# The masks of a relative bias, made by three engines instead of one, and the order of the work around them

## The reference

```python
c_act = jax.nn.silu(c)
mod = c_act @ ada_w[l] + ada_b[l]                 # 2048 -> 6 * 2048
sh_a, sc_a, g_a, sh_f, sc_f, g_f = jnp.split(mod, N_MOD, axis=-1)
h = modulate(rms_norm(x, attn_pre_norm[l]), sh_a, sc_a)      # h * (1 + sc_a) + sh_a
...
proj = h @ w_in                                    # the first large product
...
rel = positions[:, None, :] - pq[:, :, None]       # key position - query position
bias = jnp.take(bias_tab, t5_bucket(rel), axis=0)  # 32 buckets, 8 heads
s1 = (dq1 @ dk1) * DIFF_SCALE + bias               # and s2 likewise
```

## Time and profile before

| | before |
|---|---|
| median of 3 executions | 1926.73 us |
| lowest, highest | 1925.74, 1927.43 us |
| the profiled execution | 1925.74 us, its span 1924.0 us |
| busy: PE, PEld, DVE, ACT, POOL | 1772.4, 1703.6, 1242.0, 879.2, 215.9 us |
| mean granted clock of TensorE | 0.959 of full speed |
| read from memory | 372.85 MB, 195 GB/s over the span |

### The profile page before, as it was taken

One profiled execution on the slowest core, in us unless ns is written; L12 is line 12 of the kernel. 1 busy time (PEld: TensorE's weight loads), 2 busy tenths in 40 slices (PEclk: granted clock), 3 DMA queues, 4 the chain that ended last, 5 costly groups with the idle time before them and its releaser, 6 DMA issues.

```text
span 1924.0 us, 33456 instructions
## 1 busy us (share of the span) xinstructions
PE 1772.4 (92%) x13960; PEld 1703.6 (89%) x13960; DVE 1242.0 (65%) x1747; ACT 879.2 (46%) x1448; POOL 215.9 (11%) x126
## 2 busy tenths in 40 slices
PE   3799988879979999999999999999699999978997
PEld 3699986869969999999999999999599999856797
DVE  7798889473577757767767656655644446565544
ACT  8444334543445445445445445444444443464432
POOL 0243440003430000000000000000200000161000
PEclk7799999998979999999999999999899999998998
DMA  9797688446936656666656655554155554441151
GB/s 386 262 377 296 243 300 263 134 139 213 341 146 206 226 190 223 222 200 226 220 195 230 217 178 186 186 164 153 49 184 186 183 176 158 142 132 44 39 170 56
DMA packets 102822, 377.13 MB, mean 196 GB/s; under 512 B 11536, under 2 KB 11664, under 8 KB 102544
## 3 DMA queue, kind: packets, MB, share of 16 engines
q1 hardware_dynamic: 102672, 374.99, 57.2%
HBM read 372.85 MB, written 2.10 MB: 195 GB/s over the span
## 4 chain that ended last, share of the span: by engine, by line
issue 46%; PE 37%; DVE 12%; ACT 3%; POOL 1%; DMA 1%; SPq 0%; ACTq 0%; DVEq 0%; POOLq 0%
PE ps L509 10%; PE ps L510 10%; PE ps L511 10%; DVE ada_acc L1190 5%; DVE probs L1301 2%; ACT masks L966 1%; DVE stats L1275 1%; PE ps L591 1%; PE ps L547 1%; PE ps L540 1%; DVE w_lo L1175 1%; POOL probs L1669 1%; PE ps L625 1%; PE ps L610 1%; ACT w_hi L862 1%
## 5 line engine op out<-in xcount | busy, mean ns | idle before, releaser
L509 PE MATMUL ps<-h_hi,w_hi 128*128 128x256 f32 x3264 | 944.7, 289 | 22.4 <-DVE h_lo L1242 10.5
L510 PE MATMUL ps<-h_lo,w_hi 128*128 128x256 f32 x3264 | 930.2, 285 | 0.0
L511 PE MATMUL ps<-h_hi,w_lo 128*128 128x256 f32 x3264 | 929.9, 285 | 0.0
L1175 DVE TENSOR_TENSOR w_lo<-raw,w_hi 128x1024 fp32r<-128x1024 f32 x448 | 553.3, 1236 | 377.3 <-ACT w_hi L862 375.2
L862 ACT ACTIVATE w_hi<-raw 128x1024 fp32r<-128x1024 f32 x512 | 538.7, 1057 | 424.6 <-PE ps L511 404.8
L509 PEld LDWEIGHTS ps<-h_hi,w_hi 128*128 128x128 f32 x3264 | 632.7, 194 | 29.1 <-issue 15.8
L510 PEld LDWEIGHTS ps<-h_lo,w_hi 128*128 128x128 f32 x3264 | 633.8, 194 | 1.1
L511 PEld LDWEIGHTS ps<-h_hi,w_lo 128*128 128x128 f32 x3264 | 633.2, 194 | 0.0
L1190 DVE SCALAR_TENSOR_TENSOR ada_acc<-raw,c_act,ada_acc 128x1024 f32<-128x1024 f32 x180 | 257.9, 1457 | 2.1 <-DMA raw<-in_ada 1.9
L1676 POOL TENSOR_TENSOR w_lo<-raw,w_hi 128x1024 fp32r<-128x1024 f32 x64 | 171.9, 2693 | 471.6 <-ACT w_hi L862 471.6
L509 PE MATMUL ps<-g_hi,w_hi 128*128 128x256 f32 x704 | 201.1, 286 | 3.7 <-DVE g_lo L1513 3.7
(11 more groups left out here) (199 smaller groups left out, 1335.0 us busy)
## 6 DMA issues: line engine op xcount, KB each, us to landing
raw<-in_weights SPq DMA_DIRECT2D x512, 512.0 KB, 3.9
raw<-in_ada SPq DMA_DIRECT2D x192, 512.0 KB, 5.1
x<-in_x SPq DMA_DIRECT2D x1, 2048.0 KB, 17.3
out_y<-x SPq DMA_DIRECT2D x4, 512.0 KB, 2.6
consts<-in_consts SPq DMA_DIRECT2D x1, 863.5 KB, 6.3
params<-in_params SPq DMA_DIRECT2D x1, 593.5 KB, 3.8
probs<-in_pos_q SPq DMA_DIRECT2D x1, 128.0 KB, 2.1
probs<-in_pos_k SPq DMA_DIRECT2D x1, 32.0 KB, 2.4
```

What stands on the lines that cost most here:

```text
L509: nc.tensor.matmul(out, wh, hi[:, k, :], start=start, stop=False)
L510: nc.tensor.matmul(out, wh, lo[:, k, :], start=False, stop=False)
L511: last = nc.tensor.matmul(out, wl, hi[:, k, :], start=False, stop=stop)
L1175: V.tensor_tensor(w_lo[:, h % W_SLOTS, :], raw[:, raw_slot("w", h), :], w_hi[:, h % W_SLOTS, :].bitcast(F32), ALU.subtract).then_inc(lo_dv ...
```

## The change

It makes the same bias in another way. A mask is now 1 where the distance is at or past the start and 0 elsewhere, so the starts are whole numbers, the steps are no longer halved and the added column is gone. The 64 keys are split in eight blocks of eight. For blocks 0 to 4 ScalarE writes the distances in float32 (`distances`, 128x256 each, into the two halves of the later `bias`) and GpSimd compares a block with zero (128x2048). For blocks 5 to 7 VectorE compares `start` with the negated key positions in one instruction of 128x2048 (`last_masks`), set after items 1, 2 and 4 of the modulation. TensorE takes the squares of x first, then waits for the mean of x, for the exponential and for the masks, and makes the bias sums in the order 0, 3, 1, 2. ScalarE's eight `bias_out` all stand behind the root. VectorE's `lo(0)` stands behind the first `modulate`. (`lo(H_IN + 1)`, also taken out, was empty on VectorE: that half is GpSimd's.)

```diff
@@ tensor @@
-            def bias_sums(i):
-                pe.wait_ge(bias_mask, i + 1)
...
+            mean_square("x0", KT)
+            pe.wait_ge(bias_delta, 1)
+            pe.wait_ge(lam_exp, 1)
+            pe.wait_ge(mean_ready, 1)
+            for i in BIAS_GROUPS:
+                if i == 3:
+                    pe.wait_ge(last_mask, 2)
+                elif i == 2:
+                    pe.wait_ge(last_mask, 3)
+                    pe.wait_ge(bias_mask, POOL_MASKS)
+                else:
+                    pe.wait_ge(bias_mask, 2 * i + 2)
+                for qt in range(0, 2):
...
-            for i in range(3):
-                bias_sums(i)
-            pe.wait_ge(lam_exp, 1)
-            bias_sums(3)
-            pe.wait_ge(bias_ready, 6)
-            mean_square("x0", KT)
             pe.wait_ge(bias_ready, 8)
             mod_sum(0)
@@ scalar @@
-            def signs(i):
-                for k in range(16 * i, 16 * i + 16):
-                    last = nc.scalar.activation(masks[:, k, :], start, ACT.Sign, bias=pos_k[:, k:k + 1])
-                last.then_inc(bias_mask, 1)
+            def distances(b):
+                if b >= 2:
+                    act.wait_ge(bias_mask, b - 1)
+                for k in range(8):
+                    last = nc.scalar.activation(distance[b % 2][:, k, :], start, ACT.Identity,
+                                                bias=pos_k[:, 8 * b + k:8 * b + k + 1])
+                last.then_inc(distance_ready, 1)
+            act.wait_ge(start_ready, 1)
+            distances(0)
+            distances(1)
+            act.wait_ge(angle_ready, 1)
+            nc.scalar.activation(cs1[:, :, :], cs1[:, :, :], ACT.Sin).then_inc(cs_ready, 1)
+            distances(2)
+            act.wait_ge(inputs_loaded[4], 16)
+            squares("x0", KT, lambda k: x[:, k, :])
+            distances(3)
+            distances(4)
+            act.wait_ge(lam_sum, 1)
+            nc.scalar.activation(lam[:, 2:4], ps[:, OUT + 1, 0:2], ACT.Exp).then_inc(lam_exp, 1)
+            root("x0")
+            act.wait_ge(bias_mask, POOL_MASKS)
+            for n in range(8):
                 act.wait_ge(bias_summed, n + 1)
...
@@ vector @@
+            chain.link(V.tensor_scalar(neg_pos_k[:, :], pos_k[:, :], -1.0, None, ALU.mult))
...
+            def last_masks(b):
+                dve.wait_ge(start_ready, 1)
+                V.tensor_tensor(masks[:, 8 * b:8 * b + 8, :], start.unsqueeze(1).broadcast_to([P, 8, S]),
+                                neg_pos_k[:, 8 * b:8 * b + 8].unsqueeze(2).broadcast_to([P, 8, S]), ALU.is_ge
+                                ).then_inc(last_mask, 1)
...
-            chain.link(V.tensor_tensor(delta[:, 0, :], delta[:, 0, :], par("tab_last"), ALU.add))
-            chain.link(V.tensor_scalar(delta[:, 0, :], delta[:, 0, :], 0.5, None, ALU.mult))
...
             for i in range(32):
                 ada(i)
-                if i == 24:
+                if i in (1, 2, 4):
+                    last_masks({1: 6, 2: 7, 4: 5}[i])
+                elif i == 24:
...
-            lo(H_IN)
-            lo(H_IN + 1)
             mod_out(0)
             mod_out(1)
             modulate("x0", lambda k: scale_cols[:, 0, k:k + 1], SH_A, 0, SLAB)
+            lo(H_IN)
             lo(H_IN + 2)
@@ gpsimd @@
+            for b in range(POOL_MASKS):
+                pool.wait_ge(distance_ready, b + 1)
+                nc.gpsimd.tensor_scalar(masks[:, 8 * b:8 * b + 8, :], distance[b % 2], 0.0, None, ALU.is_ge
+                                        ).then_inc(bias_mask, 1)
```

More of the change, by code:

```diff
@@ L201 @@
     ("conv_w2", 2 * FF_TILES), ("k_pos", CMP_LEN), ("v_pos", CMP_LEN), ("w2k", 2 * P),
[L202 removed]
+    ("w2v", 2 * P), ("lq", 2), ("lk", 2), ("sinks", 16), ("tab_next", HEADS), ("tab_prev", HEADS))
 CONSTS, N_CONSTS = columns(
@@ L259, in build_program @@
         pos_k = sb("pos_k", [P, 64])
+        neg_pos_k = sb("neg_pos_k", [P, 64])
         probsT = sb("probsT", [P, 2, 2 * S])
@@ L309, in build_program @@
         consts_cast, zeros_ready = sem("consts_cast"), sem("zeros_ready")
-        start_ready = sem("start_ready")
+        start_ready, distance_ready = sem("start_ready"), sem("distance_ready")
+        last_mask = sem("last_mask")
         bias_mask, bias_delta, bias_summed, bias_ready = (
@@ L362, in build_program @@
         cmp_x_lo_v = [h_lo[:, 4 * w:4 * w + 4, :].rearrange("p a b -> p (a b)") for w in range(2)]
+        distance = [bias[:, b, :, :] for b in range(2)]
         latents = proj1[:, QLAT:QLAT + 6, :]
@@ L436, in build_program @@
         CMP_SPLIT = {1: 2, 2: 3, 4: 4, 5: 5, 7: 6, 9: 7, 10: 8, 13: 9}
+        BIAS_GROUPS = [0, 3, 1, 2]
+        POOL_MASKS = 5
         M_DIFF, M_MLA, M_B, M_A, M_END = 0, 16, 24, 40, 56
@@ L654, in _ @@
                              stop=True).then_inc(lam_sum, 1)
-            def bias_sums(i):
-                pe.wait_ge(bias_mask, i + 1)
-                for qt in range(2):
+            mean_square("x0", KT)
[11 more added lines that the diff above has]
+                for qt in range(0, 2):
                     for k in range(16):
                         for part in range(3):
-                            last = nc.tensor.matmul(ps[:, 4 * qt + i, 32 * k:32 * k + 32],
-                                                    masks[:, 16 * i + k, P * qt:P * qt + P], delta3[:, part, :],
-                                                    start=part == 0, stop=part == 2)
+                            last = nc.tensor.matmul(
+                                ps[:, ds(4 * qt + i, 1), 32 * k:32 * k + 32].rearrange("p a n -> p (a n)"),
+                                masks[:, 16 * i + k, ds(P * qt, P)],
+                                delta3[:, part, :], start=part == 0, stop=part == 2)
                     last.then_inc(bias_summed, 1)
-            pe.wait_ge(bias_delta, 1)
-            for i in range(3):
-                bias_sums(i)
-            pe.wait_ge(lam_exp, 1)
-            bias_sums(3)
-            pe.wait_ge(bias_ready, 6)
-            mean_square("x0", KT)
             pe.wait_ge(bias_ready, 8)
@@ L979, in bias_out @@
                 last.then_inc(bias_ready, 1)
[L981 to L994, removed]
             hi(0)
@@ L1770, in _params @@
     prev = np.concatenate([table[rows[:1]], table[rows]])
-    last = np.where(np.arange(P)[:, None] % 32 == 0, nxt[-1:], 0.0)
     lam = np.zeros((P, 4), np.float32)
@@ L1783, in _params @@
         i["cmp_v_pos_2"][0].T, w2[0], w2[1], lam,
-        np.broadcast_to(i["sinks_2"], (P, 16)), np.tile(nxt, (4, 1)), np.tile(prev, (4, 1)), last], axis=1).astype(np.float32)
+        np.broadcast_to(i["sinks_2"], (P, 16)), np.tile(nxt, (4, 1)), np.tile(prev, (4, 1))], axis=1)
 def _constants():
@@ L1802, in _constants @@
     starts = np.array([-1e9] + BUCKET_STARTS + [1e9])
-    put("start", np.tile(starts - 0.5, 4))
+    put("start", np.tile(starts, 4))
     put("prev_sign", np.tile(np.array([0.0] + [-1.0] * 31), 4))
```

3 lines of the change are left out of this document (1 added, 2 removed).

## The result

The changed kernel took 1955.57 us (median of 4 runs, 1954.48 to 1956.82) against 1926.24 us of the kernel before: a ratio of 1.0151, interval 1.0134 to 1.0169. That is 29.3 us more. Forecast were 1939.5 us and at most 1951. The sign was right; the size, +12.8 us, was less than half of what came. The profiled execution took 1954.82 us with a span of 1953.0 us, 29.0 more than the span before.

A forecast was written before the change was run, and what follows sets the result against it. Bound: VectorE behind ScalarE's signs in the opening, paced by loads, then TensorE. +9.6 us to the mean and +3.5 behind it, +13.1, on a median of 1926.73 gave 1938.8 to 1939.8; said 1939.5, range 1931 to 1951.

The forecast's parts named there:

- the cost of one mask: Opening, GpSimd: one 128x2048 one-input comparison priced near a copy, 1.9 us plus a quarter, taken as 2.4 us.
- 10.8 us ahead of the mean: Opening, VectorE before item 24: five GpSimd masks cost it 5 x (2.4 - 0.25) = 10.8 us.
- not 12.1: From the mean of x to TensorE's modulation sums: bias sums 10.8 us plus hand-overs 1.2, start 12.1 us after the mean.
- safe upper bound: Opening, GpSimd: a mask costs at most the two-input price, 4.8 us; as a rival 1951 us, chance 0.10.
- Its length less 0.25: Opening, VectorE: each GpSimd mask falling before item 24 costs VectorE the mask's length less 0.25 us.
- GpSimd gets in behind the running operation, always: Opening: GpSimd waits only for the VectorE operation that runs, then VectorE stands for GpSimd's length less about 0.25 us.
- still before item 24: Opening, ScalarE: distances, squares and the last masks end by about 47 us, hidden before VectorE's item 24 at 60.9.
- 3.71 us became 6.99: TensorE's modulation sums: taken as 3.71 us at granted clock 1.00 instead of 6.96 at 0.50, 3.25 us won.
- the extra 7.9 us from the last modulation sum taken up to the first product: VectorE to TensorE: last sum taken up at 78.05 us, first product 7.9 us later at 85.95.
- unit 0 at the lower clock: TensorE, unit 0: after some 8 us of rest, 24 products at 0.21 us each, 5.1 us, ending about 91.05.
- w_lo(0) as a term of its own: VectorE: w_lo of half 0 stands behind all the modulation, adding 1.21 us; TensorE starts after it, not under the modulation.
- SyncE's loads without effect in stage A: SyncE's queue: loads go out later, at about 86 us, but count nothing; up to 4 us if the cover fails.

The follow-up runs named there:

- the bursts: Separate kernel without the reference's work: ten bursts of fourteen VectorE items, one GpSimd operation asked for in each; GpSimd's comparison took 6.25 us in the first, 13.41 once.
- k6b: Kernel before, squares of x ahead of most bias sums, one bias-sum group held back until 31 items are done: 1925.16 us, ratio 0.9990.
- k6c: Kernel before, squares of x ahead of the bias sums, two bias-sum groups held back until 29 items are done: 1922.95 us, ratio 0.9981.
- k7: Kernel before with only VectorE's w_lo of half 0 moved behind the modulation: 1931.63 us, ratio 1.0020.
- k5: Changed kernel with all eight comparisons on VectorE, no masks on GpSimd and no distances on ScalarE: 1948.71 us, ratio 1.0100.
- k1: Changed kernel with VectorE's w_lo of half 0 put back ahead of the modulation: 1947.70 us, ratio 1.0106.
- k6d: Kernel before with the changed kernel's TensorE order (squares, then all bias sums behind the mean), masks on ScalarE, w_lo of half 0 early: 1927.48 us, ratio 0.9998.
- k6: Kernel before with squares of x moved ahead of most bias sums, one bias-sum group behind the mean, masks on ScalarE: 1924.13 us, ratio 0.9986.
- 32 bursts: Separate kernel without the reference's work: bursts of 18 VectorE items, one GpSimd operation asked for behind a given item; let in at most at the eighth item.
- first measurement: Separate kernel without the reference's work: GpSimd operations alone (comparison 5.36 us, cast 1.89), then ten bursts of fourteen VectorE items with one GpSimd operation each.
- k3: Changed kernel with one wait more, VectorE's item 12 waiting for item 11: 1955.61 us (one run).

## Why the prediction was wrong, point by point

The steps that failed are the cost of one mask ("take 2.4", measured 5.36 us) and the path by which the masks act: the sum let them cost VectorE 10.8 us ahead of the mean and nothing behind it. Two of the five cost VectorE 8.7 us ahead of the mean, and the other three, of which GpSimd could not begin the first for 32 us, held up the copies of the bias, so that the modulation sums began 24.1 us after the mean and not 12.1.

- **The length of a mask (the step that failed first).** I put a one-input comparison beside the copies and allowed a quarter more: 2.4 us, bounds 1.9 to 4.8. It is 5.36. The lower bound was right for a cast and meant nothing for arithmetic; what I took for a safe upper bound, the two-input price, lies below the one-input price (4.49 against 5.36 for 2048 elements).
- **What a mask costs VectorE.** "Its length less 0.25" fits w_lo, where a two-input item stood 2.1 us beside 2.34, but not a mask: beside 5.36 us the item stood 3.4. One-input work stood to the mask's end: the copy of the bursts for 5.21 us, and in the changed kernel the short steps L1390 and L1394 right behind the two-input ones, which is why the first two masks cost 8.7 / 2 = 4.35 us each. The Trainium skill's page "SBUF — State Buffer" (Who interferes with whom) has the lock held for the whole instruction; by these runs two-input operations come back after about two thirds of the mask. In any case one mask let in cost VectorE 3.4 to 4.35 us, and the comparison done on VectorE itself 2.2.
- **Who waits.** I assumed that GpSimd gets in behind the running operation, always. The overlaps of the earlier trace rows show just that. In the changed kernel the third mask met the ninth operation of a run of 33, and was shut out to its end. Part of the loss that I put on the mean (61.35, measured 58.50) came back on the masks: the modulation sums started 24.1 us after the mean and not 12.1.
- **What else hung on the masks.** The distances and the bias share a tile, so the copies wait for the last mask, and Exp stands behind distances that wait for the third. I had costed both as hidden ("still before item 24"), which could be true only of short masks that get in. VectorE's last seven items hung on them too: they waited for Exp until 68.24 us, stood 3.4 us beside the fifth mask (8.25 us for four) and ended at 78.45 + 3.57 = 82.0, only 0.5 us before the last copy (75.16 + 7.39 = 82.55). To free the copies alone would have gained hardly more than that.
- **The modulation sums.** 3.71 us became 6.99. I let the clock stand over a hand-over. It did not stand: it fell to 0.50 in a pause of 1.12 us in one kernel and of 4.37 in another, and was at 1.00 for most of the sums in the two kernels without one (k6b, k6c).
- **Right:** the extra 7.9 us from the last modulation sum taken up to the first product (97.50 - 89.69 = 7.8), unit 0 at the lower clock (5.1), 2.88 us per unit after it, w_lo(0) as a term of its own (k7: 4.8 us at unit 0), SyncE's loads without effect in stage A (unit 30 is as late as unit 0).

At unit 0 the errors add up: -2.85 at the mean, +12.0 to the modulation sums, +2.5 over them, -0.1 after, together 11.5 (102.58 - 91.05). Another 4.4 us come behind the opening, which I had at nothing. They arise in small steps. 3.3 us of them lie between 254 and 282 us of the kernel before, and of these 1.8 are one row of eight products, which took 3.80 us at a granted clock of 0.50 and before 2.01 at 1.00. By the medians k5 shows 4.3 us behind the opening too (21.5 against 17.2), though the eight products took 2.01 there, k1 only 1.0 (21.2 against 20.2), and k7 nothing (4.4 against 4.8). Single executions of one kernel lie several us apart, so what makes these steps was not settled.

The opening's 24.6 us by experiments: 0.6 for the order (k6d), 4.5 for w_lo(0) (k1), 7.5 for the masks on GpSimd instead of VectorE (k5), and the rest, 12.0, for masks on VectorE instead of ScalarE. No experiment changes this last item alone, but k5 and k6d bear it out: their modulation sums begin at 74.84 and 63.29 us, 11.6 apart, with nothing of w_lo(0) in it. The gain that the order could bring is 3.0 to 4.5 us at unit 0 (k6, k6c), and it needs none of the other edits.

A warning about luck: with 5.36 in place of 2.4 my formula, 5 x (5.36 - 0.25), gives 1954, close to the measured time. It would have been right for a wrong reason, with the mean at 76 us.

## What to carry to other kernels

Price an engine's operation from the same kind of operation (copy, one-input arithmetic, two inputs), and if no row shows that kind, let the range hold more than the dearest neighbour. Before moving work from a waiting engine to GpSimd, compare what it takes from VectorE while it runs with what it would cost VectorE to do it, look whether VectorE ever pauses, and follow what waits for the last piece, not only for the first. Short TensorE work that hangs on the clock is best put directly behind other TensorE work that has brought the clock up, without a hand-over.

## What the runs showed of the hardware

- GpSimd, 128x2048 float32 in: cast 1.89 us, one-input compare or multiply 5.36, two-input subtract 4.49; the compare of 1024 elements 2.77, about half. The Trainium skill's page "GPSIMD Engine Reference" (section 4.1) calls one-input work roughly line-rate; of the operations measured here the cast (0.92 ns per element) comes near that, one-input arithmetic (2.6 ns) does not.
- GpSimd waited 32 us for VectorE's operations to pause (26.46 to 58.0, and the mask ended 5.4 later). The limit was eight operations since the last pause in all 32 bursts, but not in two bursts of the first measurement and not beside operations with an input from PSUM; a pause of 0.1 us (items 1.39 us apart instead of 1.20) ended the wait.
- TensorE stood 2.04 and 2.63 us among the bias sums in k6d, 1.94 in k5, 1.82 in k6c and 1.61 in k3, for no wait in the profile, but not at all in the changed kernel, where the same 384 products ran through in 9.93 us. The loads do not sort the cases: in k5 they were at full rate meanwhile (DMA share 1.01 from 66 to 68 us), in k6d's second stop hardly any ran (0.11 from 58 to 60), and the changed kernel ran through at 0.92 (76 to 78). The cause is open.
